# Quarter products from the fifth up block on, scaled x kept, and sums of weight quarters on VectorE

## The reference

```python
xl = layer_norm(ALPHA * xl + ml[2] * dl, p["ln1_g"], p["ln1_b"])
fl = sq_relu_mlp(modulate(xl, ml[3], ml[4]), p["w_up"], p["w_down"])   # square(relu(h @ w_up)) @ w_down
xl = layer_norm(ALPHA * xl + ml[5] * fl, p["ln2_g"], p["ln2_b"])       # the same for the context tokens xc
```

## Time and profile before

| | |
|---|---|
| median of 3 runs | 1601.22 us (1600.44 to 1601.52) |
| the profiled execution: its own time, its span | 1601.32 us, 1598.9 us |
| PE, DVE, ACT, POOL busy | 1461.9, 1083.0, 543.3, 305.2 us |
| mean granted TensorE clock | 0.967 |

### The profile page before, as it was taken

One profiled execution on the slowest core, in us unless ns is written; L12 is line 12 of the kernel. 1 busy time (PEld: TensorE's weight loads), 2 busy tenths in 40 slices (PEclk: granted clock), 3 DMA queues, 4 the chain that ended last, 5 costly groups with the idle time before them and its releaser, 6 DMA issues.

```text
span 1598.9 us, 23573 instructions
## 1 busy us (share of the span) xinstructions
PE 1461.9 (91%) x9102; PEld 1291.2 (81%) x9102; DVE 1083.0 (68%) x1670; ACT 543.3 (34%) x987; POOL 305.2 (19%) x263
## 2 busy tenths in 40 slices
PE   4899999989898999999999679889989999999945
PEld 3799999756688888999899469768889889988934
DVE  2693455677457966766677885935896677666798
ACT  2333333266426422332223144242642223322300
POOL 1200000010103132212321510000322322132152
PEclk8999999999999999999999879999999999999977
DMA  9421233466723212322224221451322223222501
GB/s 317 129 80 54 80 106 113 139 206 205 257 80 119 74 59 80 106 80 66 86 85 153 98 70 62 156 169 53 119 80 79 80 80 97 67 73 79 197 27 66
DMA packets 130656, 172.79 MB, mean 108 GB/s; under 512 B 3635, under 2 KB 103339, under 8 KB 130563
## 3 DMA queue, kind: packets, MB, share of 16 engines
q1 hardware_dynamic: 123106, 146.57, 28.4%
q0 software_dynamic: 6640, 22.29, 4.2%
q10 hardware_dynamic: 816, 2.65, 0.4%
HBM read 162.58 MB, written 8.91 MB: 107 GB/s over the span
## 4 chain that ended last, share of the span: by engine, by line
PE 73%; DVE 17%; issue 3%; DMA 3%; ACT 3%; POOL 1%; SPq 0%; DVEq 0%; ACTq 0%; POOLq 0%
PE ps L718 35%; PE ps L1204 21%; PE ps L700 4%; DVE wlo L1734 3%; PE ps L751 2%; PE ps L709 1%; DMA ln_gb<-in_ln_b_l 1%; PE ps L950 1%; PE ps L1047 1%; DVE p_pad L2411 1%; PE ps L927 1%; PE ps L1070 1%; DVE h_lo L2200 1%; DVE ln_small L2186 1%; DMA raw<-in_w_mod_l 1%
## 5 line engine op out<-in xcount | busy, mean ns | idle before, releaser
L1307 ACT ACTIVATE whi<-raw 128x512 fp32r<-128x512 f32 (+2 forms) x204 | 189.1, 936 | 443.1 <-PE ps L718 362.2
L718 PE MATMUL ps<-whi,hid_hi 128*128 128x512 f32 x640 | 253.5, 396 | 40.5 <-DVE wlo L1734 21.8
L1734 DVE TENSOR_TENSOR wlo<-raw,whi 128x512 fp32r<-128x512 f32 (+2 forms) x204 | 261.1, 1288 | 42.7 <-ACT whi L1307 38.5
L718 PE MATMUL ps<-wlo,hid_hi 128*128 128x512 f32 x640 | 252.2, 394 | 0.0
L718 PE MATMUL ps<-whi,hid_lo 128*128 128x512 f32 x640 | 251.7, 393 | 0.0
L718 PEld LDWEIGHTS ps<-whi,hid_hi 128*128 128x128 f32 x640 | 122.1, 191 | 67.2 <-DVE wlo L1734 22.6
L2156 DVE TENSOR_TENSOR acc<-acc,ps 128x512 f32<-128x512 f32 x120 | 79.9, 683 | 130.2 <-PE ps L718 130.2
L718 PE MATMUL ps<-whi,h_hi 128*128 128x256 f32 (+1 forms) x480 | 157.5, 328 | 7.6 <-DVE wlo L1734 6.1
L718 PE MATMUL ps<-whi,h_lo 128*128 128x256 f32 (+1 forms) x480 | 153.4, 320 | 0.0
L718 PE MATMUL ps<-wlo,h_hi 128*128 128x256 f32 (+1 forms) x480 | 153.2, 319 | 0.0
L1204 PE MATMUL ps<-t_hi,whi 128*128 128x320 f32 x448 | 138.9, 310 | 5.4 <-DVE h_hi L2245 5.4
(11 more groups left out here) (303 smaller groups left out, 2926.7 us busy)
## 6 DMA issues: line engine op xcount, KB each, us to landing
raw<-in_w_mod_l SPq DMA_DIRECT2D x43, 1024.0 KB, 5.2
raw<-in_w_up_l SPq DMA_DIRECT2D x32, 1024.0 KB, 5.4
raw<-in_w_down_l SPq DMA_DIRECT2D x32, 1024.0 KB, 5.1
raw<-in_w_in_l SPq DMA_DIRECT2D x15, 1024.0 KB, 5.3
raw<-in_w_out_l SPq DMA_DIRECT2D x8, 1024.0 KB, 5.1
raw_more<-in_w_mod_l SPq DMA_DIRECT2D x5, 1024.0 KB, 10.0
x_spill<-x_tok POOLq DMA_DIRECT2D x10, 512.0 KB, 8.6
x_tok<-x_spill POOLq DMA_DIRECT2D x10, 512.0 KB, 6.1
```

The lines of the kernel that those rows point to most:

```text
L718: mm = pe.matmul(out, a_of(still, k), w_of(part, k), start=(first and k == 0 and part == 0 and still == 0), stop=(last and k == nk - 1 and ...
L1307: act.activation(ring_piece(whi, w, g), piece(w, g), ACT.Copy).then_inc(hi_done, 1)
L1734: dve.tensor_tensor(ring_piece(wlo, w, g), piece(w, g), ring_piece(whi, w, g).bitcast(F32), ALU.subtract).then_inc(lo_done, 1)
```

## The change

- Quarter products start with up block 4 (`SU = 4`); blocks 2 and 3 are computed plainly, 96 matmuls of 320 columns each (`weights_still`), with `relu_square` on ACT and `square_low` on DVE.
- `weight_sums` runs on DVE, one block ahead. `token_sums` and `low_t` move behind blocks 2 and 3.
- x is scaled on DVE (`rescale`) during the second half of blocks 0 and 1 and in block 2, and stored after that. The gains for it are loaded before the MLP (`load_gb(0)`, `load_gb(2)`). After the last up block x and the gains of the second LayerNorm are fetched (`fetch_x_again`); nothing is scaled there.
- `gated_sum` works at full width, and each tile's follows at once on that tile's group of down 13.
- GpSimd keeps its DMA issues and the one-column operations of the norms.

```diff
-            return kind == "up" and n >= 2
+            return kind == "up" and n >= SU
...
@@ gpsimd
-            def weight_sums(layer, u, i=None):
...
-            def fetch_normed(layer):
+            def fetch_x_again(layer):
+                pool.wait_ge(up_mm[layer], CONV_UP + NS_UP * NPROD)
                 pool.wait_ge(x_re, 16 * NT * (2 * layer + 2))
                 for t in range(NT):
                     pool.dma_start(x[:, t, :], A["x_spill"][t * P:(t + 1) * P, :]).then_inc(x_re, 16)
-                load_gb(2 * layer)
-            def scale_x(layer):
...
+                load_gb(2 * layer + 1)
@@ tensor
             def up(layer, u, i=None):
+                if u < SU:
+                    pe.wait_ge(lo_done, OPS[w + 1])
+                    for m in range(2):
+                        n = 2 * u + m
+                        pe.wait_ge(relu_ok[layer], 8 * layer + n - 1)
+                        b = 2 * (n % 2)
+                        weights_still((bank(b, 0, HALF), bank(b + 1, 0, HALF)), w_cols(w, BW, m * P, P),
+                                      h_cols(HP), KT).then_inc(up_mm[layer], 1)
+                    return
@@ scalar
+            def relu_square(layer, n):
+                act.wait_ge(up_mm[layer], n + 1)
+                if n >= 6:
+                    act.wait_ge(sq_lo[layer], n - 1)
+                r = tmp[:, n % 2, 0:TOK]
+                act.activation(r.rearrange("p (b n) -> p b n", b=2), two(2 * (n % 2)), ACT.Relu).then_inc(relu_ok[layer], 1)
+                act.wait_ge(relu_ok[layer], 8 * layer + n + 1)
+                act.activation(uhi[:, n, :], r, ACT.Square).then_inc(sq_hi[layer], 1)
@@ vector
-            def gated_sum(layer, d, t):
+            def gated_sum(layer, t):
+                if t == 0:
+                    dve.wait_ge(x_re, 16 * NT * (2 * layer + 3))
+                dve.wait_ge(acc_ok[layer], 65 + t + 1)
+                mark(dve.tensor_tensor(acc[:, t, :], acc[:, t, :], gate[:, 0, int(t == LAT), :], ALU.mult))
+                settle()
+                dve.scalar_tensor_tensor(x[:, t, :], x[:, t, :], ALPHA, acc[:, t, :],
                                          ALU.mult, ALU.add).then_inc(acc_pre[layer], 1)
+            def weight_sums(w, i=None):
...
+                raw_ready(dve, w_k[w], i)
...
+                dve.tensor_tensor(s1, a21, a22, ALU.add).then_inc(sums, 1)
+                dve.wait_ge(sums, lin(c + 1, 16, i))
+                dve.tensor_tensor(s2, s1, a11, ALU.subtract).then_inc(sums, 1)
+                dve.tensor_tensor(a21, a11, a21, ALU.subtract).then_inc(sums, 1)
...
+                dve.wait_ge(sums, lin(c + 2, 16, i))
+                dve.tensor_tensor(s4, a12, s2, ALU.subtract).then_inc(sums, 1)
@@ vector, up_step(layer, u, i, late)
                 if late:
                     split_lo(w, i, (3, 4, 5))
                 if two_ups:
+                    weight_sums(w + 1, i)
                     split_lo(w + 1, i, (0,))
@@ vector, mlp(layer)
-                token_sums(layer)
                 for n, (f, hf) in enumerate(FIRST):
                     first_low(layer, f, hf)
...
                     if n == 5:
-                        split_lo(W_UP[layer] + 2, None, (0, 1, 2))
+                        split_lo(W_UP[layer] + 2)
+                    if n >= 4:
+                        rescale(2 * layer, n - 4)
...
+                    if kind == "up":
+                        split_lo(w + 1)
+                        square_low(layer, 2 * n)
+                        if n == 2:
+                            rescale(2 * layer, 4)
+                        else:
+                            low_t(layer, 0, 4, 1, tlo[:, 0])
+                            low_t(layer, 1, 0, 0, tlo[:, 1])
+                        square_low(layer, 2 * n + 1)
+                        if n == 2:
+                            token_sums(layer)
+                        else:
+                            low_t(layer, 2, 0, 1, hhi[:, 0:4, HALF:TOK])
+                            low_t(layer, 3, 4, 0, hlo[:, 0:4, HALF:TOK])
+                            dve.wait_ge(t_lo, 4 * (layer + 1))
+                        continue
                     late = True
+                    if strassen(w + 1):
+                        weight_sums(w + 1, i)
                     split_lo(w + 1, i, (0, 1, 2) if strassen(w + 1) else None)
                     for t in range(NT):
                         down_group(layer, n, t, i)
-                    if n == 12:
-                        rescale(2 * layer, 0)
-                        rescale(2 * layer, 1)
-                    if n == 13:
-                        for t in range(NT):
-                            gated_sum(layer, 12, t)
-                            gated_sum(layer, 13, t)
+                        if n == 13:
+                            gated_sum(layer, t)
```

More of the change, by code:

```diff
@@ L621, in spill_x @@
                 for t in range(NT):
-                    pool.wait_ge(ln_n, 2 * NT * layer + t + 1)
+                    pool.wait_ge(ln_x, 2 * NT * layer + t + 1)
                     pool.dma_start(A["x_spill"][t * P:(t + 1) * P, :], x[:, t, :]).then_inc(x_re, 16)
-            def weight_sums(layer, u, i=None):
[L627 to L643, removed]
-            def fetch_normed(layer):
-                pool.wait_ge(up_mm[layer], 4 + 14 * NPROD)
+            def fetch_x_again(layer):
+                pool.wait_ge(up_mm[layer], CONV_UP + NS_UP * NPROD)
                 pool.wait_ge(x_re, 16 * NT * (2 * layer + 2))
@@ L650, in fetch_normed @@
                     pool.dma_start(x[:, t, :], A["x_spill"][t * P:(t + 1) * P, :]).then_inc(x_re, 16)
-                load_gb(2 * layer)
-            def scale_x(layer):
[L655 to L661, removed]
+                load_gb(2 * layer + 1)
             def mlp(layer):
                 spill_x(layer)
[L666 to L673, removed]
+                fetch_x_again(layer)
+            load_gb(0)
             norm_share(0)
             mlp(0)
-            pool.wait_ge(acc_pre[0], 2 * NT)
+            pool.wait_ge(acc_pre[0], NT)
             pool.memset(ub[:], 0.0).then_inc(zeros, 1)
@@ L1579, in first_relu @@
                 cols = slice(hf * HALF, (hf + 1) * HALF)
-                c = 4 * layer + n + 1
+                c = (8 if hf else 4) * layer + n + 1
                 act.wait_ge(up_mm[layer] if hf else up_h0[layer], n + 1 if hf else c)
@@ L1613, in mlp @@
                     first_relu(layer, f, hf)
[L1614 to L1619, removed]
                     if n == 5:
-                        split_hi(W_UP[layer] + 2, None, (0, 1, 2))
-                late = True
+                        split_hi(W_UP[layer] + 2)
+                late = False
                 for kind, n, i in mlp_steps(act):
@@ L1627, in mlp @@
                         late = True
+                        continue
+                    if n < SU:
+                        split_hi(w + 1)
+                        relu_square(layer, 2 * n)
+                        if n == 3:
+                            for m, (k0, hf) in enumerate(((4, 1), (0, 0), (0, 1), (4, 0))):
+                                high_t(layer, m, k0, hf)
+                        relu_square(layer, 2 * n + 1)
                         continue
```

83 lines of the change are left out of this document (42 added, 41 removed).

## The result

The changed kernel takes 1554.92 us (median of 4 runs, 1553.25 to 1555.98); the kernel before took 1601.37 us beside it. The ratio is 0.971, with a 95% interval of 0.9693 to 0.9727: 46.5 us faster. 1552.8 us was forecast, with a range of 1547.5 to 1562.0. The profiled execution took 1555.98 us, 45.3 us less than that of before, and its span is 1554.2 us.

The account below looks back on a forecast made before the run. PE's own work and idle times set the end. 4.05 + 3.66 + 19.6 + 19.95 + 1.2 = 48.5 us gained, so 1601.3 - 48.5 = 1552.8 us; own range 1549 to 1556, 8 in 10 range 1547.5 to 1562.

Parts of the forecast that it names:

- Start of the MLP: First half unit to down 0: PE starts down 0 earlier, by 4.05 us in layer 0 and 3.66 in layer 1.
- the margins of 0.4, 2.3 and 1.0 us: MLP start: inputs ready before PE wants them: `h_lo` by 0.4, split of down 0 by 2.3, first add by 1.0.
- More PE work: Four blocks going back to plain: 48 matmuls more, 7.05 us, all on the path, 3.52 a layer.
- steady part: Up and down blocks with the weight sums on DVE: costs 0, upper bound 13 us in 12 pairs.
- The price of a sum: Sum of weight quarters on DVE: 0.69 us, 2.6 us for four with one dependent step.
- the margin of 2.5 us: Even up block: DVE's first `combine` ends at +6.3 us, PE wants the bank at +8.8.
- B: Up blocks: DVE sets the pace if a sum costs 1.54 us; 1566, or 1588 with slow matmuls; chance 0.06.
- C: Up blocks: sums of 1.8 us each make 12 pairs cost PE 4.0 us each, eating the gain; chance 0.02.
- End of the MLP: Down 12 to down 15: PE idles 2.5 us instead of 20.3; 19.6 us gained in layer 0, 19.95 in layer 1.
- rival D: MLP end: `gated_sum` waits for fetched x, the 10.90 us stay in both layers, 18 us lost, 1571; chance 0.05.
- The term of 1.2 us: Slow matmuls behind the idle time before down 15: 1.2 us gained in layer 0, none in layer 1; bounds 0 and +4.7.

Follow-up runs that it names:

- after_again: The changed kernel timed once more with no edit: 1553.67 us, ratio 0.9702 of the kernel before.
- sums_gpsimd: Changed kernel with the sums of weight quarters (`weight_sums`) back on GpSimd, all else as changed: 1561.21 us, ratio 0.9747 of the kernel before.
- sums_gpsimd_held: Changed kernel with weight sums on GpSimd, each layer's first held until DVE has added down 0's five groups: 1554.47 us, ratio 0.9708 of the kernel before.
- token_sums_first: Changed kernel with the token sums back at the start of the MLP, before DVE's first squares: 1558.91 us, ratio 0.972 of the kernel before.
- more_dve8: Changed kernel with eight unused DVE operations added behind the sums of each even up block from up 4: 1592.47 us, ratio 0.9942 of the kernel before.
- before_scale_dve: Kernel before, with all five tiles of x scaled on DVE behind down 12 and none on GpSimd: 1596.93 us, ratio 0.9964 of the kernel before.
- gated_behind: Changed kernel with the five full-width gated sums behind all groups of down 13: 1569.84 us, ratio 0.9797 of the kernel before.
- split_first: Changed kernel with the split of down 15 moved before the gated sum of token tile 4: 1550.12 us, ratio 0.9672 of the kernel before.

## Why the prediction was right, and where it missed

**Start of the MLP.** Right: 3.76 and 3.5 us gained where 4.05 and 3.66 were forecast, and 4.05 in layer 0 of `after_again`. The `h_lo` wait at the second half of blocks 0 and 1 is gone, and `h_lo` takes 1.23 us, as an operation with nothing beside it. PE has no idle time from 508.31 on, so the margins of 0.4, 2.3 and 1.0 us held. The one of 1.0 us is real, and measured 1.5: `sums_gpsimd` overran it, `sums_gpsimd_held` restored it. That moving `token_sums` is part of the gain is shown by `token_sums_first`; the share of the plain blocks themselves was not tried alone.

**More PE work, steady part.** Right: 48 matmuls, at the pace read from the earlier trace rows; 311.16 us as before. The price of a sum, 0.69 us from the nearest row of DVE, measured 0.68; the margin of 2.5 us measured 2.4 to 2.5. Rivals B and C need sums of 1.3 and 1.8 us; `more_dve8` shows that their mechanism exists and what it costs, so they fell by the size of a sum alone. GpSimd's 1.5 us was the wrong row for it: it is another engine's.

**End of the MLP.** Right to 0.1 us: 35.15 was counted and 35.15 and 35.16 measured. Its parts are separately shown: `before_scale_dve` for the sharing of DVE's and GpSimd's time (9.44 to 6.30 us; the rest of that idle time is gone where nothing is scaled there, in `gated_behind` too), `gated_behind` for the place of the gated sums (rival D's consequence, 16 us of its 18). The fetched x was not late.

**The clock.** The term of 1.2 us fits this pair: behind 903.89, 48 matmuls took 12.68 us, behind 924.09 of before 14.09, a gain of 1.4, and in layer 1 nothing (12 matmuls took 4.64 us behind 1513.60 and as much before). But `after_again` has 11.20 us for the same 48 behind an idle time of the same length, a gain of 2.9. So the bounds were the right thing to give, and the value in them was partly chance. Where `split_first` leaves next to no idle time, the clock stays at full speed in both layers:

```profile
901.60:903.60 2.00, 2.00 (x9) 1.00 0.41 106
1511.20:1513.20 2.00, 2.00 (x11) 1.00 0.00 0
```

There the 18 matmuls take 4.2 us in each layer, against 7.1 and 5.8 before the change: 4.5 of the 4.7 us come back. By the rule of the Trainium skill (TensorE: Matmul & The Clock Gate, What's actually happening) alone, every idle time that is taken away gives its slow matmuls back, the whole 4.7 us. These traces agree for an idle time that is gone; one that is only cut to 2.49 us gave back 1.4 or 2.9 us in layer 0 and nothing in layer 1.

**The range.** The range of the forecast alone, 1549 to 1556, has a slip. The clock term of 1.2 us lies between 0 and 4.7, which is -3.5 and +1.2 on the time, or 1549.3 to 1554.0; the +2 and the upper end of 1556 are not worked out anywhere. The median of 1554.92 lies between the two, so this narrow range held only by an end that the sum does not give. The wide one, 1547.5 to 1562, held in any case.

**Where it missed.** The sum is 3.2 us too large against the profiled execution (2.0 against the median), because the start of the program, taken as 0, cost 3.17 us there. It is the attention stage, and neither the sum nor a rival had a term for it. The timelines of PE there, first before, then after:

```profile
331.24 1.07 PE L751 MATMUL ps<-raw,cpad 128*32 128x256 f32 x16 [2.13 <-DMA raw<-in_w_mod_l]
...
357.11 1.07 PE L751 MATMUL ps<-raw,cpad 128*32 128x256 f32 x16 [1.39 <-DMA raw<-in_w_mod_l]
```

```profile
332.40 1.07 PE L715 MATMUL ps<-raw,cpad 128*32 128x256 f32 x16 [2.79 <-DMA raw<-in_w_mod_l]
333.40 1.42 PE L1022 MATMUL ps<-head,e_att 128*128 128x128 f32 x6
334.62 2.64 PE L1034 MATMUL ps<-v_tok,pT 128*128 128x128 f32 x12
...
359.92 1.07 PE L715 MATMUL ps<-raw,cpad 128*32 128x256 f32 x16 [1.41 <-DMA raw<-in_w_mod_l]
```

PE waits there for loads of `w_mod`, the weights that the modulation is computed from, 2.79 us in place of 2.13, and the 18 matmuls behind take 1.7 us longer than those of before (the granted clock is 0.72 from 332 to 338, and 1.00 from 331 to 337 in the kernel before); 2.8 of the 3.2 us are lost by 359.92. The change adds nothing before 438.88, where GpSimd issues the early load of the gains, and the start varies between executions: the first half unit came at 498.02 and 496.28 in the two profiles of the changed kernel, at 495.27 to 501.49 in the eight profiles of its variants, and at 500.62 in a variant of the kernel before, whose own profile has the earliest, 494.85. So the forecast was made against the shortest front of all these executions, which is a matter of chance. What makes these loads late was not tried, and with two profiles of the kernel before and its variant it stays open whether the front is later on average in the changed kernel.

## What to carry to other kernels

Where two engines work side by side, compare the duration of one operation alone and beside the other before you split work between them: here DVE alone scaled five tiles sooner than DVE and GpSimd did together. A stage that is full on the bounding engine can take work on another engine up to its tightest margin, and that margin can be counted from rows and measured by doses of dummy work; look for it where the stage begins, not only where it repeats. Independent work that stands ahead of a needed operation in an in-order stream becomes idle time of the engine that waits for it; put the needed one first. Look then at the next wait behind: part of the gain may end there.

## What the runs showed that was not expected

- After idle times of one length PE's matmuls are sometimes slow and sometimes not, even in the same program. Behind 2.59 us at 498.02 ten matmuls of 320 columns stood 0.27 us apart, behind 2.55 us at 496.28 in `after_again` none did. Behind 2.49 us at 903.89, 48 matmuls of 512 columns took 12.68 us, in `after_again` 11.20. Such a cost can only be given as a range.
- When DVE and GpSimd both work from SBUF, both get slower: in `sums_gpsimd`, GpSimd's 128x512 sum took 1.29 us where DVE rested or added from PSUM, and 2.15 to 2.54 beside DVE's splits and `low_t`; DVE's split of 128x2048 elements took 2.35 and 4.43.
- The stores of x landed after 2.9 us each when issued one at a time (median), where the five at once of the kernel before took 8.6.
